# Six weight chunks loaded as 120 and 8 rows, phase ends copied out by halves, and residual rows entering behind the third pair

## The reference

```python
q = jnp.einsum('nd,de->ne', xb, w_q).reshape(n, PEER_HEADS, 2, PEER_HALF)
s = jnp.einsum('nhie,ike->nhik', q, keys)
top_s, top_i = lax.top_k(s, PEER_TOPK)
...
best_s, best_pos = lax.top_k(cand_s, PEER_TOPK)
idx = jnp.take_along_axis(cand_i, best_pos, axis=-1)
gate = jax.nn.softmax(best_s, axis=-1)
u = expert_u[idx]
act = jax.nn.gelu(jnp.einsum('nhkd,nd->nhk', u, xb), approximate=False)
coef = (gate * act).astype(xb.dtype)
return jnp.einsum('nhk,nhkd->nd', coef, expert_v[idx])
```

## Time and profile before

| | |
|---|---|
| median of three runs | 1629.3 us |
| profiled execution | 1629.12 us, span 1627.3 us |
| busy share of PE, DVE, ACT, GpSimd (POOL) | 74%, 72%, 32%, 37% |
| moved by DMA | 665 MB, 409 GB/s over the span |
| granted TensorE clock, mean | 0.88 |

### The profile page before, as it was taken

How to read it: one execution, slowest core, us unless ns; L and a number is a source line. 1 busy time by engine, 2 the same in 40 slices (tenths; PEclk the granted TensorE clock), 3 DMA queues, 4 the chain that set the end, 5 groups by cost and what they waited for, 6 DMA issues and landing times.

```text
span 1627.3 us, 21833 instructions
## 1 busy us (share of the span) xinstructions
PE 1202.7 (74%) x7488; PEld 591.0 (36%) x7488; DVE 1171.0 (72%) x3339; ACT 527.0 (32%) x1231; POOL 600.7 (37%) x542
## 2 busy tenths in 40 slices
PE   8876786868748887978687788799697855555565
PEld 3661232225415663533264355444234611111111
DVE  4479768668768687786677866788956886666665
ACT  0222143222224564642132355455311232222221
POOL 1034433533334244233333323441433345444442
PEclk9998897989879998998898799999798988777767
DMA  9879999999999999999999999999999989999997
GB/s 380 339 297 412 423 421 421 422 421 421 421 417 415 423 425 420 420 423 422 422 422 422 384 424 424 421 421 417 395 414 424 416 354 421 422 421 421 421 421 315
DMA packets 84079, 665.05 MB, mean 409 GB/s; under 512 B 9376, under 2 KB 9392, under 8 KB 11008
## 3 DMA queue, kind: packets, MB, share of 16 engines
q0 software_dynamic: 74752, 540.13, 80.3%
q1 hardware_dynamic: 9216, 123.53, 18.0%
HBM read 662.57 MB, written 1.05 MB: 408 GB/s over the span
## 4 chain that ended last, share of the span: by engine, by line
DMA 29%; PE 29%; DVE 26%; ACT 7%; issue 7%; POOL 2%; another core or an unknown queue 0%; DVEq 0%; POOLq 0%; ACTq 0%; SPq 0%
DMA ring<-in_experts,idx 28%; PE acc L928 11%; DVE ring L1584 9%; PE act_bank L610 7%; PE dve_bank L596 6%; DVE h L1390 2%; DVE onehot L1219 2%; DVE scratch L1219 2%; POOL ring L500 2%; ACT diag L1148 1%; ACT L990 1%; ACT h L1070 1%; PE act_bank L596 1%; ACT scratch L990 1%; PE act_bank L890 1%
## 5 line engine op out<-in xcount | busy, mean ns | idle before, releaser
L500 POOL DMA_INDIRECT ring<-in_experts,idx x510 | 573.5, 1125 | 947.6 <-PE acc L928 732.0
L928 PE MATMUL acc<-ring,diag 64*64 64x512 f32 x4080 | 608.2, 720 | 315.8 <-ACT diag L1148 307.9
L1584 DVE CUSTOM_DVE_ANT_0 ring<-ring,hn 128x1024 f32<-128x1024 f32 x512 | 620.7, 1224 | 220.1 <-DMA ring<-in_experts,idx 197.1
L928 PEld LDWEIGHTS acc<-ring,diag 64*64 64x64 f32 x4080 | 155.1, 153 | 665.2 <-ACT diag L1148 427.2
L1141 ACT ACTIVATE acts<-dots 128x2 f32<-128x2 f32 x256 | 52.1, 203 | 674.6 <-DVE dots L1584 642.2
L610 PE MATMUL act_bank<-hnT,wbuf 128*128 128x128 f32 x1728 | 218.0, 284 | 23.3 <-ACT h L1070 19.5
L1148 ACT ACTIVATE diag<-cst,coefs 128x64 f32<-128x64 f32 x512 | 150.3, 340 | 252.1 <-DVE coefs L1592 215.4
L610 PEld LDWEIGHTS act_bank<-hnT,wbuf 128*128 128x128 f32 x1728 | 205.2, 197 | 70.1 <-issue 63.0
L990 ACT ACT_TABLE_LOAD x80 | 102.6, 1283 | 19.4 <-DMA rowc<-in_rows 17.0
L1592 DVE TENSOR_TENSOR coefs<-acts,gate 128x2 f32<-128x2 f32 x256 | 42.7, 167 | 79.5 <-ACT acts L1141 64.7
L1141 ACT ACT_TABLE_LOAD x68 | 87.2, 1283 | 6.2 <-DVE dots L1584 0.3
(11 more groups left out here) (173 smaller groups left out, 1024.8 us busy)
## 6 DMA issues: line engine op xcount, KB each, us to landing
wbuf<-in_weights SPq DMA_DIRECT2D x48, 2048.0 KB
ring<-in_weights SPq DMA_DIRECT2D x7, 2048.0 KB, 19.4
ring<-in_experts,idx POOLq DMA_INDIRECT x510
kept<-in_weights SPq DMA_DIRECT2D x2, 2048.0 KB, 21.8
wbuf<-in_weights SPq DMA_DIRECT2D x2, 1024.0 KB, 7.0
scratch<-in_bias POOLq DMA_DIRECT2D x1, 1024.0 KB, 12.0
scratch<-in_bands POOLq DMA_DIRECT2D x1, 768.0 KB, 13.3
h<-in_x SPq DMA_DIRECT2D x1, 512.0 KB, 3.7
```

The lines of the kernel that those rows point to most:

```text
L500: pool.indirect_dma_start(ring[:, n % RING], None, io[f"experts{layer}"], bass.IndirectOffsetOnAxis(idx[:, at:at + 1], 0),).then_inc(sem(f ...
L928: last[rows] = pe.matmul(acc[rows][half][home:home + HALF_P], diag[part, n % DIAGS], ring[part, slot, D + half * CW:D + (half + 1) * CW], ...
L1584: dve.tensor_tensor_reduce(out=ring[:, slot, 0:D], in0=ring[:, slot, 0:D], in1=hn[:, phase % NBLK], scale=1.0, scalar=0.0, op0=ALU.mult, o ...
```

## The change

It has four parts.

1. Of the chunks that go to `wbuf`, six (numbers 12, 19, 26, 33, 40, 47) are loaded by two DMAs instead of one: rows 0 to 119, and rows 120 to 127. A DMA of 128 rows spreads over sixteen DMA engines with 8 rows each, one of 120 rows over fifteen with 8 each, one of 8 rows over eight with one each. PE waits for both (`chunk_landed`).
2. At a phase end ACT tells after each half of the columns (`odd_copied`), and DVE copies the even halves out of `acc` as they are (`copy_even`, no wait for ACT) and tells after each half (`even_copied`). PE starts half 0 of pair 0 once half 0 is copied by both, then half 1. One addition of `odd_sums` to `h` follows after the dot of slot 3 (`add_odd`). `take_stream` moves from before pair 0 to behind the third pair (TAKEN_AT = 7).
3. In each phase the eight PE products that spread the norm's gain over the partitions (`gain_rows`) move from behind head 0's scores to before head 0's queries.
4. The routing of head 1 in phases 1 to 3: its part 1 moves from slot 2 to slot 4. In phase 0, two instead of three heads are searched (and two instead of three scored ahead of the first exponential) before slot 0, and the searches of the rest come one per slot.

```diff
+LOADED = sum(kind == "wbuf" for kind, _ in HOMES)
+PARTED = range(12, LOADED, 7)
+WIDE = 120
+def chunk_landed(n):
+    return 16 * (n // NWB + 1 + sum(m <= n and m % NWB == n % NWB for m in PARTED))
...
-EARLY_HEADS, ROUTED_HEADS = 6, 3
+EARLY_HEADS, ROUTED_HEADS = 6, 2
+TAKEN_AT = 3 * GROUP + 1
+ROUTE_FROM = 4
...
-            ROUTE_DUE.append(max(_due, _part) if _head else _due)
-TOPS_FIRST = 3
-TOPS_DUE = [-3, -2, -2, 0, 1, 1, 3, 5]
+            if _head == 1:
+                _due = max(_due, _phase * SLOTS + ROUTE_FROM + _part - 1) if _phase and _part else max(_due, _part)
+            ROUTE_DUE.append(_due)
+TOPS_FIRST = 2
+TOPS_DUE = [-3, -2, 0, 1, 2, 3, 4, 5]
...
-                            sp.dma_start(wbuf[:, n % NWB].rearrange("p k c -> p (k c)"), w
-                                         ).then_inc(sem(f"chunk_in{n % NWB}"), 16)
+                            into = wbuf[:, n % NWB].rearrange("p k c -> p (k c)")
+                            if n in PARTED:
+                                sp.dma_start(into[0:WIDE], w[0:WIDE]).then_inc(sem(f"chunk_in{n % NWB}"), 16)
+                                sp.dma_start(into[WIDE:P], w[WIDE:P]).then_inc(sem(f"chunk_in{n % NWB}"), 16)
+                            else:
+                                sp.dma_start(into, w).then_inc(sem(f"chunk_in{n % NWB}"), 16)
...
+                for half in range(2):
+                    out = fill("dve")
+                    for j in range(4):
+                        row = layer * KD + 4 * half + j
+                        ins = pe.matmul(out[:, j * P:(j + 1) * P], ident[:, row:row + 1].to_broadcast([P, P]),
+                                        gain_rows, start=True, stop=True)
+                    ins.then_inc(sem("dve_full"), 1)
...
                         ins = pe.matmul(acc[rows][half][part], folded[part],
                                         h[part, phase % NBLK, half * CW:(half + 1) * CW],
-                                        start=True, stop=False, skip_group_check=True)
+                                        start=False, stop=False, skip_group_check=True)
...
                 for half in range(2):
+                    if start and g:
+                        pe.wait_ge(sem("even_copied"), 2 * (g // STEPS - 1) + half + 1)
+                        pe.wait_ge(sem("odd_copied"), 2 * (g // STEPS - 1) + half + 1)
...
-                    if n == GROUP:
-                        if phase:
-                            pe.wait_ge(sem("acc_read"), phase)
-                            pe.wait_ge(sem("odd_copied"), phase)
-                        take_stream(phase)
...
+                    if n == TAKEN_AT:
+                        take_stream(phase)
...
-            def read_acc(phase):
+            def copy_even(phase):
                 for rows in range(2):
                     dve.wait_ge(sem(f"pairs_summed{rows}"), (phase + 1) * STEPS * GROUPS + AHEAD)
-                lane.need("odd_copied")
                 for half in range(2):
                     for rows in range(2):
                         part = slice(rows * HALF_P, (rows + 1) * HALF_P)
                         cols = slice(half * CW, (half + 1) * CW)
-                        started = lane.start(dve.tensor_tensor(h[part, phase % NBLK, cols], odd_sums[part, cols],
-                                                               acc[rows][half][part], ALU.add))
-                lane.after(started)
-                lane.tell("acc_read")
+                        started = lane.start(dve.tensor_copy(h[part, phase % NBLK, cols], acc[rows][half][part]))
+                    lane.after(started)
+                    lane.tell("even_copied")
+            def add_odd(phase):
+                for half in range(2):
+                    lane.need("odd_copied")
+                tt(h[:, phase % NBLK], h[:, phase % NBLK], odd_sums, ALU.add)
...
                     if n == GROUP and phase:
-                        read_acc(phase - 1)
+                        copy_even(phase - 1)
+                    if n == GROUP + 1 and phase:
+                        add_odd(phase - 1)
```

More of the change, by code:

```diff
@@ L579, in next_chunk @@
                     return staged[:, at].rearrange("p (k c) -> p k c", k=KD)
-                pe.wait_ge(sem(f"chunk_in{n % NWB}"), 16 * (n // NWB + 1))
+                pe.wait_ge(sem(f"chunk_in{n % NWB}"), chunk_landed(n))
                 return wbuf[:, n % NWB]
@@ L892, in queries @@
                     ins.then_inc(sem("act_full"), 1)
[L893 to L901, removed]
             def side(layer, b):
@@ L929, in sum_pair @@
                                                    ring[part, slot, D + half * CW:D + (half + 1) * CW],
-                                                   start=start and odd == 1, stop=stop, skip_group_check=True)
+                                                   start=start, stop=stop, skip_group_check=True)
                 for rows in range(2):
@@ L1161, in copy_odd @@
                                                             acc[rows][half][home], ACT.Copy))
-                lane.after(started)
-                lane.tell("odd_copied")
+                    lane.after(started)
+                    lane.tell("odd_copied")
             def move_last_odd():
```

## The result

The changed kernel took 1688.7 us (median of four runs, 1687.48 to 1690.21), the kernel before in the same session 1630.01 us (1629.07 to 1631.11): a ratio of 1.036, 95% interval 1.0342 to 1.0378. The change costs 58.7 us, where 8.0 us of gain were forecast. The profiled execution took 1687.55 us.

What follows compares the result with a forecast made beforehand. The prediction took DMA, behind the start the load of one slow engine, to bound the kernel. 5.5 us from the split loads plus 2.5 from the start made 8.0 off 1629.1: 1621.1 us, range 1617.3 to 1627.6.

Steps and rivals of the forecast that it cites:

- the step that failed: Six loads as 120 and 8 rows: relieve the engine that is behind, 5.5 us gained, between 1.5 and 7.2.
- the uneven split is slower: Rival, six loads: two engines write through one memory entrance; 5.0 us lost per load if time doubles; chance 0.07.
- point of decision: Six loads: the split's price that cancels the 8.0 us gain, 1.3 us a load, 27% slower.
- the slow engine: End of phase 2: one DMA engine works on alone, 9.2 us behind the others; taken to be number 15.
- the slow engine was not spared: Sign of being wrong, behind the last phase end: a busy share of 0.06 again, one engine working alone.
- the 29.9 us: Six loads: DMA time taken off the last engine, which gets no rows of 120; 5.0 us a chunk.
- the 5.5 us: Six loads: 9.2 us the next slowest engine idled, less 3.7 for its extra rows.
- What bounds the kernel: Behind the start: DMA at 421 GB/s, set by the load of the one engine that is behind.
- worth 0: Phase ends: shorter waits alone gain nothing, as the engine behind never ran dry; bound 5.2 us.
- 2.5 us taken: Start, 112 to 120 us: PE's moved products let a gather issue earlier; 2.5 us gained, between 0 and 4.6.
- by slot 5, so pair 2 gains little: Start: DVE's moved searches return by slot 5, so pair 2, on which the seventeenth gather waits, gains little.

Runs made afterwards that it cites:

- with no gather beside: Kernel before with seven chunks of the start loaded as 120 and 8 rows, later loads whole: 1665.43 us, ratio 1.0223.
- part 1 alone: Kernel before with only the six chunks loaded as 120 and 8 rows: 1685.22 us, ratio 1.0343.
- the phase ends alone: Kernel before with only the phase ends copied out by halves, residual rows behind the third pair and later head 1 routing: 1629.97 us, ratio 0.9996.
- all of parts 2 to 4: Changed kernel with all chunks loaded whole as 128 rows again: 1632.62 us, ratio 1.0017 to the kernel before.
- its two halves: Kernel before with only the phase ends and later head 1 routing: 1629.97 us, 0.9996; with only the start's changes: 1631.29 us, 1.0007.

## Why the prediction was wrong

**Part 1 is the step that failed.** It costed the six loads by bytes and by engines alone, "a chunk of 128 rows gives each engine 8 rows of 16 KB", and 120 rows gave fifteen of them the same 8: 0 us for the load itself. Measured, such a load costs 9.2 us. Each of the four cuts by rows has a price, 5.8 to 9.2 us, the cut by columns none, and while a load of 120 and 8 rows is in flight everything moves at about half the rate (213 to 246 GB/s). This was the rival "the uneven split is slower", at a chance of 0.07 and a price of at most 5.0 us a load, "if they take twice that". They do with no gather beside (5.1 us each), but gathers beside them slow down as well, which nearly doubles the price. The rival's point of decision, 1.3 us a load, was right and far exceeded. "No row shows a DMA of other than 128 rows" should have weighed as a cost of unknown size on a kernel bound by DMA; it was taken for nothing likely.

That two engines meet at one entrance of SBUF is what the runs suggest, not what they show: shown is that the cut by rows makes the difference, and not the bytes, the number of DMAs, the pieces or the distances at which rows are read. The Trainium skill names the mechanism in "SBUF — State Buffer", "Door 1: The DMA port swizzle", and in "DMA: Bandwidth & Descriptors", "The descriptor swizzle", it gives for 128 rows the engine of each row, four neighbours and the four that lie 32 behind, so that each engine has an entrance of its own. No run shows how other numbers of rows lie. If neighbouring rows go to one engine, two engines share an entrance of that map, and the half rate agrees with it; the sizes of the other cuts agree in order alone.

**Whether the slow engine was spared stays open.** The step took the slow engine for the last one. With the last one spared one engine is still alone at the end of phase 2 in the kernel with part 1 alone (30 GB/s), and at the end of the program in the changed kernel (28 GB/s). That is the sign that the prediction itself named for "the slow engine was not spared", and it makes this likely. It does not show it: the alone engine may also be one that the slowed loads put behind, or the spared one, if it carries more than the 29.9 us that were taken off it. Nor is it known, then, whether the 5.5 us were to be had without the price of the split.

**What bounds the kernel** is supported by the run with the phase ends alone: the phase end's gap was closed (a share of 0.96 from 1319 to 1327 us) and the time did not move, as it should if the engine that is behind had no gap there.

**Part 2** was right: copies side by side, GpSimd's wait about 5 us (5.21), worth 0 (0.9996, together with the later routing of head 1). Only PE's sum of the pair was sized too small, 3.69 us where 1314.0 to 1316.4 had been taken, at a granted clock of 0.56 from 1360 to 1370 us. The stretch in which one engine is alone moved from the phase end to the end of the program; there it is 8 us with all of parts 2 to 4, and about four with the ends alone, where eight were expected.

**Parts 3 and 4**, 2.5 us taken "between 0 (another wait takes the place) and 4.6", are 0 or a little below: another wait did take the place, one pair later. It is ACT's order of scores, exponentials and gelu first, which the step left out, and a sum at the lower clock, 3.69 us for 1.95. The searches that come back ("by slot 5, so pair 2 gains little") then delay the coefficients after it by 2 us.

**The sum**: 55.3 us for part 1 alone and 2.7 for the rest alone make 58.0, of 58.7 measured. That parts 2 to 4 together cost 2.7 us (interval 1.3 to 4.2), and its two halves -0.7 and 1.1 by their ratios, each uncertain by about 1.5, is not explained further. None of the versions tried beats the kernel before.

## What to carry to other kernels

In a kernel that DMA bounds, cost a DMA by how its rows are cut, not only by bytes: split a load of 128 rows by columns, which was free here, and not by rows, which about halved the rate of all that was in flight. Read the rate beside the busy share; at a share of 1.01 it was 423 GB/s in one stretch (660 to 730 us) and 228 in another (1306 to 1324). Before an engine is relieved by its number, show by one run that it is the one behind.

## What was not expected of the hardware

- Two DMAs of 64 rows, with equal bytes on all sixteen engines, cost 6.9 us more than one of 128; 112 and 16 rows 6.1; 126 and 2 rows 5.8; 120 and 8 rows 9.2, of which the 8 rows have 2.9 for 128 KB (9.2 less the 6.3 of the 120 rows alone).
- A chunk cut into 3840 and 256 columns of all 128 rows, the second in pieces of 1 KB, costs nothing that can be measured (1.0001).
- While a load of 120 and 8 rows is in flight, gathers slow down with it: 213 to 246 GB/s for all together, at a share of 0.99 to 1.03. The busy share does not show it, the rate does.
